# Index attention of a two-block transformer: head pairs ordered by head with query blocks 0, 2, 1, 3, and turned probabilities copied ahead of the exponents

## The reference

```python
# index attention, for each block of 128 queries
score = einsum('bqhk,bqh->bqk', relu(qi . ki), w)     # 8 index heads
score = where(causal, score, -inf)
sel   = top_k(score, 128)                             # keys of each query
p     = softmax(where(valid, q . k[sel] * 64**-0.5, -inf))
out   = (p . v[sel]) @ w_o                            # 16 heads of 64
# cross attention: 4 heads of 64, softmax over the 256 memory tokens, no mask
```

## Time and profile before

| | us |
|---|---|
| median of 3 runs | 2050.25 |
| lowest, highest run | 2047.61, 2298.82 |
| the profiled execution, its own time | 2049.47 |
| its span, first to last instruction | 2047.6 |
| TensorE busy in the span | 1941.5 (95%) |
| VectorE, ScalarE, GpSimd busy | 739.2, 754.5, 846.9 |
| index attention, first transpose to first pass of the output projection | 851.05 to 931.5 |
| cross attention, first dots to first pass of its output projection | 1657.47 to 1675.7 |

### The profile page before, as it was taken

One profiled execution on the slowest core, in us unless ns is written; L12 is line 12 of the kernel. 1 busy time (PEld: TensorE's weight loads), 2 busy tenths in 40 slices (PEclk: granted clock), 3 DMA queues, 4 the chain that ended last, 5 costly groups with the idle time before them and its releaser, 6 DMA issues.

```text
span 2047.6 us, 24974 instructions
## 1 busy us (share of the span) xinstructions
PE 1941.5 (95%) x9547; PEld 1571.9 (77%) x9547; DVE 739.2 (36%) x1276; ACT 754.5 (37%) x1193; POOL 846.9 (41%) x416
## 2 busy tenths in 40 slices
PE   2998999999999999899999999999997989999998
PEld 1776878888888868657888888878875868888887
DVE  7983221111003388771211110010057356602621
ACT  5534252223123244673432231242386363212212
POOL 1002444444444457644444444444450444444343
PEclk8799999999999799799999999999998999999999
DMA  5113323332232212102333322343300223323321
GB/s 123 17 25 130 96 69 102 102 87 87 93 103 74 76 62 88 57 1 63 95 89 102 102 73 95 111 140 93 113 22 1 94 62 82 103 85 100 102 94 70
DMA packets 210342, 168.17 MB, mean 82 GB/s; under 512 B 19538, under 2 KB 175642, under 8 KB 210201
## 3 DMA queue, kind: packets, MB, share of 16 engines
q1 hardware_dynamic: 207392, 163.10, 27.3%
q10 hardware_dynamic: 2872, 4.04, 0.6%
HBM read 162.63 MB, written 2.13 MB: 80 GB/s over the span
## 4 chain that ended last, share of the span: by engine, by line
PE 62%; issue 20%; POOL 7%; DVE 6%; ACT 4%; SPq 0%; DMA 0%; POOLq 0%; DVEq 0%; ACTq 0%
PE PS L1898 51%; POOL w_lo L592 6%; PE PS L2153 1%; PE PS L2097 1%; PE PS L2092 1%; PE PS L2107 1%; PE PS L2137 1%; ACT probs L1113 1%; PE PS L2144 1%; DVE stay L1618 1%; PE PS L1802 1%; ACT probs_t L1120 1%; PE PS L1803 1%; PE PS L1823 1%; PE PS L1835 1%
## 5 line engine op out<-in xcount | busy, mean ns | idle before, releaser
L592 POOL TENSOR_TENSOR w_lo<-raw,w_hi 128x2048 fp32r<-128x2048 f32 x147 | 680.2, 4627 | 984.4 <-ACT w_hi L854 984.4
L854 ACT ACTIVATE w_hi<-raw 128x2048 fp32r<-128x2048 f32 x147 | 281.9, 1918 | 566.3 <-PE PS L1898 564.5
L1898 PE MATMUL PS<-xT_hi,w_hi 128*128 128x512 f32 x1104 | 430.1, 390 | 2.3 <-DVE xT_lo L1429 2.3
L1898 PE MATMUL PS<-xT_lo,w_hi 128*128 128x512 f32 x1104 | 429.5, 389 | 0.0
L1898 PE MATMUL PS<-xT_hi,w_lo 128*128 128x512 f32 x1104 | 429.5, 389 | 0.0
L1898 PEld LDWEIGHTS PS<-xT_hi,w_hi 128*128 128x128 f32 x1104 | 207.3, 188 | 46.3 <-issue 3.3
L1898 PE MATMUL PS<-w_hi,hT_hi 128*128 128x512 f32 x608 | 237.0, 390 | 5.1 <-POOL w_lo L592 5.1
L1898 PEld LDWEIGHTS PS<-xT_lo,w_hi 128*128 128x128 f32 x1104 | 207.2, 188 | 43.0
L1898 PEld LDWEIGHTS PS<-xT_hi,w_lo 128*128 128x128 f32 x1104 | 207.2, 188 | 42.8
L1898 PE MATMUL PS<-w_lo,hT_hi 128*128 128x512 f32 x608 | 236.6, 389 | 0.0
L1898 PE MATMUL PS<-w_hi,hT_lo 128*128 128x512 f32 x608 | 236.6, 389 | 0.0
(11 more groups left out here) (328 smaller groups left out, 2133.2 us busy)
## 6 DMA issues: line engine op xcount, KB each, us to landing
raw<-in_ffn_w_gate_up SPq DMA_DIRECT2D x88, 512.0 KB, 4.6
raw<-in_ffn_w_down SPq DMA_DIRECT2D x40, 512.0 KB, 4.3
raw<-in_w_up SPq DMA_DIRECT2D x32, 512.0 KB, 4.7
raw<-in_w_down SPq DMA_DIRECT2D x32, 512.0 KB, 4.3
raw<-in_dsa_w_in SPq DMA_DIRECT2D x28, 512.0 KB, 4.5
raw<-in_w_in SPq DMA_DIRECT2D x21, 512.0 KB, 5.0
raw<-in_s_w_glu SPq DMA_DIRECT2D x16, 512.0 KB, 4.6
raw<-in_dsa_w_o SPq DMA_DIRECT2D x8, 512.0 KB, 4.5
```

The lines of the kernel that those rows point to most:

```text
L592: pool.tensor_tensor(w_lo[:, par, :], raw[:, par, :], f32(w_hi[:, par, :]), ALU.subtract).then_inc(w_split, 1)
L854: act.activation(w_hi[:, par, :], raw[:, par, :], ACT.Copy).then_inc(w_rounded, 1)
L1898: ins = mm(o, a if weights_stay else c, c if weights_stay else a, start=first and n == 0, stop=last and n == 2)
```

## The change

The list of the index attention is ordered by head pair first, and within a head pair by the query blocks 0, 2, 1, 3. With that, four pairs in a row fill all 512 queries of one head pair, so the output columns are one whole row of `xT_hi` and `xT_lo` for each four pairs, in place of a quarter of four rows; where a pair's product goes in the bank is now given by the unit. The row maxima wait once for all four blocks of query norms, and the output projection's first two row blocks wait for four column groups in place of one and three. In the shared helper of ScalarE the copy of the turned pair p-2 is issued ahead of the exponents of pair p, in both attentions.

```diff
-        for b in range(TB):
-            for h in range(NH):
+        for hp in range(NH // 2):
+            for b in (0, 2, 1, 3):
                 mask = masks[:, 0, :] if b == 0 else chosen[:, BLK[b]:BLK[b] + P * (b + 1)]
-                dsa_units.append((qT[:, h // 2, P * b:P * b + P], kT[:, h // 2, 0:P * (b + 1)], mask,
-                                  [v_dsa[:, k, HD * h:HD * h + HD] for k in range(b + 1)], q_ss[:, b, h:h + 1]))
+                for h in (2 * hp, 2 * hp + 1):
+                    dsa_units.append((qT[:, hp, P * b:P * b + P], kT[:, hp, 0:P * (b + 1)], mask,
+                                      [v_dsa[:, k, HD * h:HD * h + HD] for k in range(b + 1)], q_ss[:, b, h:h + 1], P * b))
 
         def dsa_columns(x, g):
-            hp = 4 * (g % 2)
-            return x[:, hp:hp + 4, P * (g // 2):P * (g // 2) + P], PS[:, 6 + g % 2, :].rearrange("p (h q) -> p h q", q=P)
+            return x[:, g, :], PS[:, 6 + g % 2, :]
...
-                      [vx[:, m, HD * h:HD * h + HD] for m in range(2)], None)
+                      [vx[:, m, HD * h:HD * h + HD] for m in range(2)], None, P * (2 * (b % 2) + h // 2))
...
                 for p in range(n + 4):
+                    if 0 <= p - 2 < n:
+                        turned_copy(p - 2)
                     if p < n:
                         exponent(2 * p)
                         exponent(2 * p + 1)
-                    if 0 <= p - 2 < n:
-                        turned_copy(p - 2)
...
-                    dve.wait_ge(q_rstd, t // NH + 1)
+                    dve.wait_ge(q_rstd, TB)
...
-                    m, at = len(units[2 * p][3]), P * (p % 4)
+                    m, at = len(units[2 * p][3]), units[2 * p][5]
...
-            n_slot(g, g % 2, WO_PANEL, range(4), xT_hi, xT_lo, True, False, turns=[3 * KT + 1, 3 * KT + 3, last - 1, last])
+            n_slot(g, g % 2, WO_PANEL, range(4), xT_hi, xT_lo, True, False, turns=[last - 4, last - 4, last - 1, last])
```

## The result

Seven runs of each kernel: 2047.61 us before (2046.0 and up), 2040.56 us after (2037.64 to 2043.53). The ratio is 0.9966 with a 95% interval of 0.9953 to 0.9978, so about 7 us less, between 4.5 and 9.6. In the later comparisons the kernel before gave medians of 2049.48 (29 runs), 2049.81 (11) and 2048.78 (25), so 2047.61 is on its low side.

What follows compares the result with a forecast made beforehand. TensorE, busy 95% of the span, was taken as the bound, at a low clock early in the index attention. Savings of 2.8 (index attention) and 1.2 (cross attention) made 4.0 us less: 2046.2 from 2050.25, range 2041.5 to 2052.

Steps and rivals of the forecast that it cites:

- the walk: Index attention, four pairs (b = 0, 2, 1, 3) stepped through at full clock: about 9.03 us, 0.5 of it TensorE standing.
- the end: Index attention's close, no dots covering the last copies: 7.55 us from the last turn(b2), so 2.1 us added.
- the later first turn: Index attention's start: longer row maxima of b = 2 delay the first normalise, so the first turn starts 0.53 us later.
- the formula: Index attention's stage time as 72.3 + 0.406 L us, against 80.5 for the old, with 0.53 on top.
- neither takes over: Index attention: VectorE (busy 9.06 of 12.19 us) and GpSimd (6.53) were not expected to become the limit.
- Rival 2: Index attention: late exponents make a turn wait for its normalise; at one us a group more, 2054 us; chance 0.13.
- L: Index attention: us at the low clock after the first turn; 12 taken, between 6 and 16.8.
- The cross attention: All pairs have 256 keys, so only the copy's place matters: 1.2 us less, between 0 and 2.
- 0.3 us a group: Index attention: new order and copy ahead together, at equal clock, per four pairs; some 2 us in all.
- Rival 4: Index attention: transposes hold the clock low through the stage, 40 us more, 2089 us; chance 0.02.
- the term of 2.8 us for the index attention: Index attention's stage forecast at 77.7 us against 80.5; 0.9 to 5.2 us less by the length of the low clock.
- a us of difference between runs: Whole kernel: allowance for run-to-run variation within the forecast range; the lower two runs lay 2.6 apart.

Runs made afterwards that it cites:

- the order 2, 0, 1, 3: The kernel before with the copy ahead of the exponents and its query blocks taken as 2, 0, 1, 3, pairs not mixed: 2040.52 us, ratio 0.9943.
- copy-alone kernel: The kernel before with only the copy put ahead of the exponents, in both attentions, old pair order: 2042.17 us, ratio 0.9969; again 2044.61 us, 0.9979.

## Why the prediction was right or wrong

- *The bound and the walk: right in size.* Four pairs at the full clock were walked at 9.03 us and took 8.95; the end, from the last turn(b2) to the projection, at 7.55 and took 7.38 (915.27 to 922.65); the later first turn was put at 0.53 and came so exactly (6.26 from first dots to first turn, before 5.73). With the measured 9.2 us of low clock the formula gives 76.0; 75.1 was measured.
- *Where TensorE waits: wrong place.* The walk had 0.16 for the copy before turn(b1) and 0.33 before turn(b3). Measured: 0.35 before turn(b1), for the normalise, and nothing before turn(b3). The walk has no step for the normalise of b1: it let VectorE out with "neither takes over", by busy shares. But the maxima of b3 start only when both of its dots are done, and this normalise stands behind them. And ScalarE's steps follow each other 0.1 closer than their recorded durations (copy of b2 at 862.51, recorded 0.81, next start 863.21), so the copies came earlier than walked. The two errors nearly cancel, with 0.1 before turn(b0) beside them; that the group came out within 0.1 us is in part luck. Rival 2 had this mechanism, at turn(b3); it is real, but it took the place of waits that the walk had elsewhere and did not come on top of them.
- *The clock: the mechanism right, the size too small.* It does come back sooner when long pairs come early; the order 2, 0, 1, 3 showed it apart, in one execution. I took L = 12 us for the low clock after the first turn and 9.2 was measured. At 0.41 us per us this is 1.1 us. L had been placed nearer to the old value because the first turns were to come with waits between them; at the low clock there were none (TensorE busy 9.09 of 9.09).
- *The cross attention: right.* 1.2 forecast, 1.3 at equal clock; only 0.2 of it in the profiled execution.
- *What is worth what: wrong.* The prediction gave order and copy together 0.3 us a group at equal clock and never walked the copy in the old order. Measured at equal clock, from the first turn: 5.5 less by the copy, 1.65 more by the order, 3.9 less together, where 0.3 a group makes 2.4 (some 2 with the later first turn). Of the 1.5 us between, 8 x 0.08 = 0.6 is the group's 8.95 for 9.03, and 0.2 the end; the rest I have not traced.
- *Rival 4*, in which transposes hold the clock low, didn't come: from 860 on the clock is 1.00 with nearly a third of TensorE's time in transposes (2.78 of 8.95 us a group).
- *The step that failed: the term of 2.8 us for the index attention, and with it the range.* The stage gave back 4.7. Of the 1.9 us between, 1.1 is L (9.2 for 12), 0.6 the groups (8.95 for 9.03) and 0.2 the end (7.38 for 7.55); the mechanism was right in the main and these sizes were off. That alone would have left the time inside the range. The other part is "a us of difference between runs", which is 3 to 4: the stage starts anywhere from 839.6 to 846.4 in fourteen executions in which nothing ahead of it differs, and in the two compared it started 4.1 earlier, which is luck of the clock and no part of the forecast. The base of 2050.25, a median of three runs, lies 2.6 above that of the seven but only 0.4 to 1.5 above those of the later comparisons. With the same lower bounds of the terms (5.2 and 2 less) from 2050.25 and 4 us for the runs, the lower edge would have been 2039.

## What to carry to other kernels

A single buffer between two engines wants its emptying copy issued as soon as it is full; put behind other work in the same list, it closes a loop over two iterations, and reordering the work can make that loop worse. When a step is both moved and reordered, walk each edit alone. Where a wait drops the clock, look first at what TensorE does in the wait and right after it: seven unused matmuls in the wait gave the old kernel 3.6 us of stage, and five gave the copy-alone kernel 4.4 or 7.5 (75.3 for 79.7 or 82.8), where the whole change gave 4.7.

## What the runs showed of the hardware

After the first turn the clock stayed at 1.2 GHz over 14.1, 16.8 and 21.2 us of a TensorE that was busy nearly all the time with pairs of one and two key blocks (13.97 of 13.97 and 20.79 of 20.79 in two of them), over 6.2 to 9.4 with the orders that mix the blocks, and 5.3 with pairs of three blocks. I had expected the time to be about the same from run to run of one kernel; for the copy alone it was not.

Two dots of a pair, on the upper and the lower 64 partitions, are ready for their reader at about the same time: VectorE's first maximum of the pair starts 0.1 us after the next TensorE step begins (870.64 behind 870.54), as in the kernel before (919.67 behind 919.57).

Executions of one kernel differ by several us because of the clock far away from any edit. Some 150 us ahead of the changed stage it was low for 20.5 us in the profiled execution of the kernel before (669.84 to 690.32) and for 13.7 in that of the kernel after, and the stage began 4.1 us apart. For edits of a few us, the length of the stage in the trace told more than the medians.
